# Latent attention on one core: the pool's second mix among the query turns, output-projection steps between the head pairs

## What is computed

```python
def pool_mixer(u, pool_w, pool_scale):
    ...
    d = jnp.stack(outs, axis=2).astype(u.dtype)          # window means minus u, 4 groups of 128
    y = jnp.einsum('bsgc,gcd->bsgd', d, pool_w).reshape(B, S, POOL_WIDTH)
    return y * pool_scale

def blocked_attention(q, k, v):                          # 8 heads, keys of 96, values of 64
    ...
        s = jnp.einsum('bqhd,bkhd->bhqk', qi, k).astype(jnp.float32) * scale
        p = jax.nn.softmax(s, axis=-1).astype(v.dtype)
        return jnp.einsum('bhqk,bkhd->bqhd', p, v)

    x = x + jnp.concatenate([a, b], axis=-1) @ w_out_e[e]
    x = x + memory_cross_attention(rms_norm(x, xattn_norm_g[i]), mem_k, mem_v, ...)
    x = x + squared_relu_mlp(rms_norm(x, ff_norm_g[i]), w_ff1[i], w_ff2[i])
```

## Time and profile before

| | |
|---|---|
| median of 3 executions | 1904.04 us (1900.67 to 1906.61) |
| profiled execution, its own time | 1904.02 us |
| its span | 1902.2 us |
| TensorE busy | 1832.1 us, 96% of the span |
| VectorE, ScalarE, GpSimd busy | 67%, 61%, 21% |
| mean granted TensorE clock | 0.985 of 2.4 GHz |
| the piece from the first query turn to the first addition of the output projection | 116.59 to 159.86 us |

### The profile page before, as it was taken

How to read it: one execution, slowest core, us unless ns; L and a number is a source line. 1 busy time by engine, 2 the same in 40 slices (tenths; PEclk the granted TensorE clock), 3 DMA queues, 4 the chain that set the end, 5 groups by cost and what they waited for, 6 DMA issues and landing times.

```text
span 1902.2 us, 32919 instructions
## 1 busy us (share of the span) xinstructions
PE 1832.1 (96%) x11312; PEld 1614.4 (85%) x11312; DVE 1269.7 (67%) x1928; ACT 1161.7 (61%) x1893; POOL 397.8 (21%) x426
## 2 busy tenths in 40 slices
PE   7889999999889999999999999999999999999998
PEld 6768888889669888888888988889888888788887
DVE  6777685775675866666667866657566565666665
ACT  4455574644455656578737869845588454759863
POOL 1103140230140511011222031212021120541212
PEclk9999999999999999999999999999999999989999
DMA  6423365566433565665654636664666646126662
GB/s 240 142 63 122 113 191 187 186 190 193 139 101 111 173 202 184 186 186 185 216 163 126 192 119 207 193 214 126 197 186 197 207 124 203 45 79 190 187 222 75
DMA packets 86764, 312.11 MB, mean 164 GB/s; under 512 B 10368, under 2 KB 15616, under 8 KB 86400
## 3 DMA queue, kind: packets, MB, share of 16 engines
q1 hardware_dynamic: 86368, 309.01, 52.3%
q10 hardware_dynamic: 288, 1.64, 0.2%
HBM read 309.56 MB, written 1.05 MB: 163 GB/s over the span
## 4 chain that ended last, share of the span: by engine, by line
PE 88%; DVE 7%; ACT 3%; issue 2%; POOL 0%; DMA 0%; SPq 0%; ACTq 0%; DVEq 0%; POOLq 0%
PE pt L500 41%; PE pt L501 21%; PE pt L494 5%; PE pt L495 5%; PE pt L496 5%; DVE w_lo L1833 2%; PE pt L614 1%; PE pt L618 1%; PE pt L616 1%; PE pt L1143 1%; PE pt L924 1%; ACT w_hi L1254 1%; DVE in_both L1861 1%; PE pt L1046 1%; PE pt L1053 1%
## 5 line engine op out<-in xcount | busy, mean ns | idle before, releaser
L1833 DVE TENSOR_TENSOR w_lo<-raw,w_hi 128x1024 fp32r<-128x1024 f32 (+2 forms) x548 | 706.2, 1290 | 297.4 <-ACT w_hi L1254 289.5
L1254 ACT ACTIVATE w_hi<-raw 128x1024 fp32r<-128x1024 f32 (+2 forms) x548 | 598.9, 1095 | 403.6 <-PE pt L501 225.6
L500 PE MATMUL pt<-in_both,w_hi 128*128 128x512 f32 x2103 | 741.8, 398 | 0.3 <-DVE in_both L2385 0.3
L501 PE MATMUL pt<-in_both,w_lo 128*128 128x256 f32 x2103 | 590.8, 281 | 0.0
L500 PEld LDWEIGHTS pt<-in_both,w_hi 128*128 128x128 f32 x2103 | 396.8, 189 | 95.5 <-DVE w_lo L1833 0.5
L500 PE MATMUL pt<-act_both,w_hi 128*128 128x512 f32 x1309 | 463.2, 399 | 0.0
L501 PEld LDWEIGHTS pt<-in_both,w_lo 128*128 128x128 f32 x2103 | 398.9, 190 | 0.1
L501 PE MATMUL pt<-act_both,w_lo 128*128 128x256 f32 x1309 | 367.3, 281 | 0.0
L500 PEld LDWEIGHTS pt<-act_both,w_hi 128*128 128x128 f32 x1309 | 246.4, 188 | 59.2 <-issue 0.9
L501 PEld LDWEIGHTS pt<-act_both,w_lo 128*128 128x128 f32 x1309 | 247.8, 189 | 0.2
L2557 POOL TENSOR_TENSOR act_both<-scr,act_both 128x256 f32 x88 | 100.2, 1139 | 493.8 <-ACT act_both L1722 493.8
(11 more groups left out here) (322 smaller groups left out, 2268.8 us busy)
## 6 DMA issues: line engine op xcount, KB each, us to landing
raw<-in_fi SPq DMA_DIRECT2D x176, 512.0 KB, 3.7
raw<-in_ff SPq DMA_DIRECT2D x128, 512.0 KB, 3.6
raw<-in_fo SPq DMA_DIRECT2D x64, 704.0 KB, 4.1
raw<-in_dq SPq DMA_DIRECT2D x24, 512.0 KB, 3.6
raw<-in_mq SPq DMA_DIRECT2D x16, 512.0 KB, 4.2
raw<-in_mo SPq DMA_DIRECT2D x16, 512.0 KB, 4.2
raw<-in_rg_u SPq DMA_DIRECT2D x10, 512.0 KB, 3.7
raw<-in_rg_y SPq DMA_DIRECT2D x10, 512.0 KB, 3.7
```

The lines of the kernel that those rows point to most:

```text
L500: nc.tensor.matmul(pt[:, b, :], lhs_hi, both.rearrange("p t s -> p (t s)"), start=start, stop=False)
L501: return nc.tensor.matmul(pt[:, b, 0:S], lhs_lo, both[:, 0, :], start=False, stop=stop)
L1254: nc.scalar.activation(w_hi[:, u.slot(), w], raw[:, u.slot(), w], ACT.Copy).then_inc(hi_split, 1)
L1833: v.tensor_tensor(w_lo[:, u.slot(), w], raw[:, u.slot(), w], w_hi[:, u.slot(), w].bitcast(F32), ALU.subtract).then_inc(lo_split, 1)
```

## The change

TensorE's second pool mix moves from behind the second pair's scores to behind the second query turn, and the last two query turns go behind the first key turns; the scores of pairs 0 and 1 now stand together, with key turns 2 and 3 behind them. Of the output projection, chunks 0 to 3 are done first for two units (banks 0 and 1) between turns and values of the attention, and for the third unit (bank 2) in one run later. ScalarE takes exponentials and copies in pairs, and the pool's high parts move up between its query copies. VectorE's pool low parts are taken one by one among maxima and norms. Two weight splits go to later places on both engines. No arithmetic is added or left out.

```diff
-            def abreast(name, wait_src, kq, wide, step, last):
+            def abreast(name, wait_src, kq, wide, step, last, begin=0):
...
-                for j in range(wide):
+                for j in range(begin, wide):
...
             pe.wait_ge(q_roped, 1)
-            for p in range(4):
-                mla_query_turn(p)
-            pe.wait_ge(k_made, 1)
-            mla_key_turn(0)
-            mla_key_turn(1)
-            mla_scores(0)
-            mla_key_turn(2)
-            mla_key_turn(3)
-            mla_scores(1)
+            mla_query_turn(0)
+            mla_query_turn(1)
             pe.wait_ge(pool_read, 1)
             for g in range(4):
...
             mm.then_inc(mixed, 1)
+            pe.wait_ge(k_made, 1)
+            mla_key_turn(0)
+            mla_key_turn(1)
+            mla_query_turn(2)
+            mla_query_turn(3)
+            mla_scores(0)
+            mla_scores(1)
+            mla_key_turn(2)
+            mla_key_turn(3)
             mla_scores(2)
             mla_turn(0)
             mla_turn(1)
...
             mla_value(0)
             mla_turn(2)
             mla_turn(3)
+            pe.wait_ge(exp_ready, h_mla + 6)
+            out_e_abreast(0, 0, 2)
             mla_value(1)
+            out_e_abreast(1, 0, 2)
             mla_turn(4)
             mla_turn(5)
+            out_e_abreast(2, 0, 2)
+            mla_value(2)
+            out_e_abreast(3, 0, 2)
+            mla_turn(6)
+            mla_turn(7)
             pe.wait_ge(exp_ready, h_mla + 7)
-            out_e_abreast(0)
-            mla_value(2)
-            mla_turn(6)
-            out_e_abreast(1)
-            mla_turn(7)
-            out_e_abreast(2)
-            out_e_abreast(3)
+            for k in range(4):
+                out_e_abreast(k, 2, 3)
+            mla_value(3)
             out_e_abreast(4)
-            mla_value(3)
             out_e_abreast(5)
             out_e_abreast(6)
```

VectorE's stream behind the first two key copies is now:

```diff
+            pool_low(0)
             mla_maxes(0)
             mla_maxes(1)
+            pool_low(1)
+            mla_maxes(2)
+            mla_norms(0)
+            mla_maxes(3)
+            mla_norms(1)
+            pool_low(2)
+            pool_low(3)
+            mla_norms(2)
+            mla_maxes(4)
+            mla_norms(3)
+            mla_maxes(5)
+            split(Pos(UNIT0["uq"] + RING))
+            mla_maxes(6)
+            mla_norms(4)
+            mla_maxes(7)
+            mla_norms(5)
+            mla_low(0)
             mla_norms(6)
             mla_norms(7)
             mla_low(1)
+            split(Pos(UNIT0["uq"] + RING + 1))
             mla_low(2)
+            split(Pos(UNIT0["uq"] + RING + 2))
             mla_low(3)
```

More of the change, by code:

```diff
@@ L868, in mla_value, with out_e_abreast @@
                 mm.then_inc(heads_out, 2)
-            def out_e_abreast(k):
-                abreast("out_e", from_act("pool"), k, 3,
-                        lambda b, hi, lo, kq, start, stop: halves(b, hi, lo, act_both[:, kq], start, stop), False)
+            def out_e_abreast(k, begin=0, wide=3):
+                abreast("out_e", from_act("pool"), k, wide,
+                        lambda b, hi, lo, kq, start, stop: halves(b, hi, lo, act_both[:, kq], start, stop), False, begin)
             pe.wait_ge(q_roped, 1)
-            for p in range(4):
-                mla_query_turn(p)
-            pe.wait_ge(k_made, 1)
-            mla_key_turn(0)
-            mla_key_turn(1)
-            mla_scores(0)
-            mla_key_turn(2)
-            mla_key_turn(3)
-            mla_scores(1)
+            mla_query_turn(0)
+            mla_query_turn(1)
             pe.wait_ge(pool_read, 1)
@@ L1530, in mla_high @@
                 nc.scalar.activation(act_hi[:, 4 + p, :], mla_out(p), ACT.Copy).then_inc(act_hi_ready, 1)
[L1532 to L1541, removed]
+            mla_query_dims(0)
+            mla_query_dims(1)
             act.wait_ge(mixed, 2)
@@ L1545, in _ @@
                                      ACT.Copy, scale=gain("ps", g)).then_inc(act_hi_ready, 1)
-            split(Pos(UNIT0["uq"] + RING))
[L1547 to L1553, removed]
+            mla_query_dims(2)
+            mla_query_dims(3)
+            mla_exps(0)
+            mla_exps(1)
+            mla_exps(2)
+            mla_key_dims(2)
+            mla_key_dims(3)
+            mla_exps(3)
+            split(Pos(UNIT0["uq"] + RING))
+            mla_copy(0)
+            mla_copy(1)
+            mla_exps(4)
+            mla_exps(5)
+            mla_copy(2)
+            mla_copy(3)
+            mla_exps(6)
+            mla_exps(7)
+            mla_high(0)
+            mla_copy(4)
+            mla_copy(5)
+            mla_high(1)
+            split(Pos(UNIT0["uq"] + RING + 1))
             mla_copy(6)
@@ L2213, in mla_low, with pool_low @@
                                 ).then_inc(act_ready, 1)
+            def pool_low(g):
+                dve.wait_ge(act_hi_ready, ACT0["pool"] + 2 + g // 2 * 2)
+                v.scalar_tensor_tensor(out=act_lo[:, g, :], in0=pt[:, 6 + g // 2, (g % 2) * S:(g % 2) * S + S],
+                                       scalar=gain("ps", g), in1=act_hi[:, g, :].bitcast(F32),
+                                       op0=ALU.mult, op1=ALU.subtract).then_inc(act_ready, 1)
             mla_key_dims(0)
             mla_key_dims(1)
+            pool_low(0)
             mla_maxes(0)
             mla_maxes(1)
[L2219 to L2232, removed]
+            pool_low(1)
[15 more added lines that the diff above has]
+            mla_low(0)
             mla_norms(6)
```

## The result

| | before | changed |
|---|---|---|
| median of the runs | 1905.19 us (4 runs, 1900.67 to 1906.61) | 1890.94 us (4 runs, 1888.58 to 1893.34) |
| ratio | | 0.993, 95% interval 0.9914 to 0.9946 |
| profiled execution | 1904.02 us | 1893.34 us |
| its span | 1902.2 us | 1891.5 us |
| first query turn to first addition, "the piece" | 43.27 us | 30.34 us |

The forecast was 1890.5 us, with 1887 to 1897 as its range. The medians differ by 14.25 us; by the interval of the ratio the gain is 10 to 16 us. In the two profiled executions the piece fell by 12.93 us, where the layout had 13.5.

A forecast was written before the change was run, and what follows sets the result against it. Latent attention was taken as bound by waits going round between engines, not by one engine. First addition moves from 159.86 to 146.3, 13.5 us less; 1904.0 − 13.5 = 1890.5 us, range 1887 to 1897.

The forecast's parts named there:

- the layout: New order from first query turn to first addition, each instruction at the later of engine free and input there; 13.5 us less.
- The claim: At VectorE's first addition of the output projection (159.86 us): a shift of this start shifts the kernel's end by as much.
- Head: First query turns to first exponential: pool mix and high parts early; first exponential at about 122.9, costing 0.5 us.
- The waits before: Old latent attention: waits go round between engines; VectorE 5.29 us for pool high parts, TensorE 1.48 for head 2's norm.
- Middle: From 122.9: ScalarE almost without wait to 136.1; TensorE's one large gap 1.5 us before pair 2's scores; value 1 to 135.0.
- tight meetings: Two meetings within 0.3 us on TensorE: value 1 with its copy, third output steps with the split of unit 2.
- The rival of a mis-sized wait: At the tight meetings: ScalarE's chain 2 to 4 us longer than laid out, 1893 to 1894.5 us; chance 0.12.
- Tail and sum: From 135.0 TensorE is full for 11.2 us; first addition at 146.3 instead of 159.86, so 13.5 us less.
- The clock: In the piece: no loss taken for clock falls in the new order; about 1 us of the gain is the old half clock.
- the swallowed gain: Behind the piece: next projection waits for weights, not VectorE's units, so time stays 1904 us; chance 0.03.
- one fall of the clock: In the new piece: one half-clock stretch as long as before, 6.3 us lost, 1896.8 us; chance 0.12.
- the slower one: First turns to first addition all at 1.2 GHz: addition at 169, 9 us later, 1913 us; chance 0.02.

## Why the prediction was right

*The claim* that the end follows the first addition held: the piece became 12.9 us shorter and 197.5 us behind it all of this was still there; of a delay of 3.7 us put in, all but 0.25 was. The times agree (14.25 us less), but their interval of 10 to 16 us would not have shown it to a microsecond.

*Head.* Forecast 0.5 us lost until the first exponential. Measured from the first query turn: 122.59 − 116.17 = 6.42, against 122.42 − 116.59 = 5.83, so 0.6.

*The waits before.* The mechanism was read rightly, but the waits of TensorE that the prediction named were not its longest. Those were 1.67 us for the pool's low parts, in front of value 0, and 2.02 us for the norm of head 4:

```profile
134.32 1.08 PE L866 MATMUL pt<-scr,big 128*64 128x256 f32 x8 [1.67 <-DVE act_both L2227]
...
144.23 1.11 PE L854 MATMUL pt<-con,spare 128*128 128x128 f32 x4 [2.02 <-DVE spare L2206]
```

*Middle.* The one gap, forecast at 1.5 us for ScalarE's key copy, was 1.41 for that copy. Both tight meetings were kept: value 1 shows no idle time in brackets, and the split of unit 2 ended at 138.67 + 1.22 = 139.89, in front of the third steps at 140.09. The rival of a mis-sized wait did not come true.

*Tail and sum.* 29.7 us by the layout, 30.34 measured; about half of the difference had come up by the end of value 1 (134.89, or 18.7 us from the first query turn, where the layout had 18.4). What was sized too low is the change from one kind of matmul to another: the step behind value 1 takes 135.35 − 134.89 = 0.46 us to the next start and not 0.35. There are six such steps, behind turns or values, at 0.43 or 0.46, 0.57 us above the price in all. Turns 4 to 7, priced at 0.44 each, took 0.40 (135.70 to 136.49 and 139.30 to 140.09 for two), which makes up for part of it.

*The clock.* Taking nothing for it was right: 1.00 from 115 to 150. The "about 1 us" for the old fall came out at 0.86 in the run with filling matmuls. The transposes did not lower it: the changed kernel has pairs of turns in every window from 125 to 140, at full rate (1.03 to 1.09 us for a pair, where half clock took 1.11 for one turn in the trace of before). By the rule that the prediction cites from the Trainium skill ("TensorE: Matmul & The Clock Gate", Part 4: PE-mode transpose) they would not have helped to hold the clock. Other matmuls stand beside them in each of these windows, so no run here can decide on that rule.

*Of the rivals*, the swallowed gain is excluded by the two traces at 197.5 us and by the delay, one fall of the clock and the slower one by the windows.

*Luck.* That 1890.5 us stands beside a measured 1890.94 is in part luck. The forecast started from 1904.04 us, and the median of before is now 1905.19; runs of one kernel differ by some 5 us; and falls of the clock behind the piece took 5 us in one trace and not in the other. What was really foretold is the piece, 13.5 against 12.93 us.

What the prediction did not say is that its parts only pay together, partly because each leaves the others' waits on the way, partly because two of them clash when they stand alone. Its sum was made for the whole order at once, so it did not need this; a sum of single gains would have come to 6 us.

## What to carry to other kernels

When waits go round between engines that each keep to their order, taking out the longest one uncovers the next in the same queue: lay out the whole new order, with starts and ends from the trace, and do not add up single gains. Check such a layout by letting it reproduce the old timeline first, and make sure that it holds the order that was built. When a part is taken out to see what it is worth, look in the timeline for waits that the taking out has made itself. Measure a change of 10 us in 1900 in its own piece, and show apart that what follows moves with it, by the same instruction in both traces and not by the times alone.

## What the runs showed that I had not expected

The same instruction streams before and behind the piece did not take the same time in the profiled executions: the first query turn started between 116.17 and 118.25 us, and from the first addition to the end of the span it was 1740.99 to 1749.21 us. With an unchanged program there, this spread of 8 us is as large as most effects looked for here; falls of the clock are one part of it, 5 us by the two places in the result above.

Half clock for 13.6 us cost only 0.86 us where TensorE waits anyway. In the run with filling matmuls some 3 us of it in the output steps made the stretch from turn 6 to the first addition 161.69 − 151.09 = 10.60 us, against 159.86 − 150.81 = 9.05 before, and with it the piece longer than before (43.96 against 43.27). It matters where the clock falls, not only for how long.
